# The norm scaling of the scan's head groups, in two halves over items 3 and 4 of the next group

## What is computed

```python
    def finish(yf, yb, xs, z):
        bb, ll = xs.shape[:2]
        y = (yf + flip(yb)).astype(xs.dtype) + xs * d_skip[:, None]
        y = y.reshape(bb, ll, SSD_D_INNER) * jax.nn.silu(z)
        y = rms_norm(y.reshape(bb, ll, SSD_N_GROUPS, SSD_D_INNER // SSD_N_GROUPS),
                     norm_g.reshape(SSD_N_GROUPS, SSD_D_INNER // SSD_N_GROUPS))
        return y.reshape(bb, ll, SSD_D_INNER) @ w_out
```

## Time and profile before

| | us |
|---|---|
| median of 3 runs | 1709.88 |
| the runs | 1709.17 to 1709.90 |
| the profiled execution | 1711.01 |
| its span | 1709.2 |
| TensorE busy | 1544.9 (90%) |
| VectorE busy | 621.9 (36%) |
| ScalarE busy | 373.4 (22%) |
| GpSimd busy | 213.0 (12%) |

### The profile page before, as it was taken

One profiled execution on the slowest core, in us unless ns is written; L12 is line 12 of the kernel. 1 busy time (PEld: TensorE's weight loads), 2 busy tenths in 40 slices (PEclk: granted clock), 3 DMA queues, 4 the chain that ended last, 5 costly groups with the idle time before them and its releaser, 6 DMA issues.

```text
span 1709.2 us, 21638 instructions
## 1 busy us (share of the span) xinstructions
PE 1544.9 (90%) x8512; PEld 788.5 (46%) x8512; DVE 621.9 (36%) x1314; ACT 373.4 (22%) x766; POOL 213.0 (12%) x232
## 2 busy tenths in 40 slices
PE   5999999999999899999888787899999998888886
PEld 2444444555444455545444353445565554444343
DVE  2533447888733414312111111748423211111112
ACT  2311148888610100000000000228210000000000
POOL 2000002222210011010101012111001010101001
PEclk9999999999999999999999999999999999999999
DMA  9687658933489799999999999942599999999997
GB/s 372 253 319 292 256 216 222 321 123 135 145 272 290 251 377 426 425 423 426 425 428 425 428 426 421 355 173 74 218 351 427 423 427 425 425 427 426 426 427 303
DMA packets 145618, 572.71 MB, mean 335 GB/s; under 512 B 23775, under 2 KB 80623, under 8 KB 114688
## 3 DMA queue, kind: packets, MB, share of 16 engines
q1 hardware_dynamic: 124928, 525.25, 77.1%
q0 software_dynamic: 14560, 25.76, 4.2%
q10 hardware_dynamic: 6048, 20.58, 3.5%
HBM read 543.02 MB, written 49.25 MB: 347 GB/s over the span
## 4 chain that ended last, share of the span: by engine, by line
PE 58%; DMA 32%; DVE 6%; issue 2%; ACT 1%; POOL 0%; SPq 0%; ACTq 0%; DVEq 0%; POOLq 0%
DMA mem<-in_moe_w_down_dram 19%; PE bank L2077 13%; DMA mem<-in_moe_w_gate_dram 12%; PE bank L648 9%; PE bank L2092 8%; PE bank L1017 6%; PE bank L962 4%; PE bank L2545 3%; PE bank L386 2%; PE bank L2655 2%; PE bank L984 1%; PE bank L995 1%; DVE mem L1193 1%; PE bank L2063 1%; PE bank L2592 1%
## 5 line engine op out<-in xcount | busy, mean ns | idle before, releaser
L2077 PE MATMUL bank<-mem 128*64 128x256 f32 x4096 | 495.5, 393 | 62.7 <-DMA mem<-in_moe_w_gate_dram 37.5
L2077 PEld LDWEIGHTS bank<-mem 128*64 128x64 f32 x4096 | 284.2, 135 | 271.3 <-DMA mem<-in_moe_w_gate_dram 59.8
L2092 PE MATMUL bank<-mem 128*64 128x512 f32 x1040 | 244.5, 613 | 41.3 <-DMA mem<-in_moe_w_down_dram 37.9
L648 PE MATMUL bank<-mem 128*128 128x512 f32 x384 | 171.2, 598 | 0.2 <-DMA mem<-in_ssd_w_in_dram 0.2
L2278 ACT ACTIVATE mem<-bank 128x256 f32<-128x256 f32 x65 | 24.9, 383 | 662.9 <-PE bank L2077 634.1
L2014 POOL DMA_INDIRECT ys_dram<-mem x61 | 61.2, 1003 | 736.7 <-DVE mem L2360 715.9
L2092 PEld LDWEIGHTS bank<-mem 128*64 128x64 f32 x1040 | 72.5, 140 | 173.7 <-issue 123.4
L2360 DVE TENSOR_TENSOR mem<-bank,mem 128x512 f32<-128x512 f32 x65 | 45.0, 692 | 226.0 <-PE bank L2092 176.0
L2339 DVE TENSOR_TENSOR mem<-mem,bank 128x256 f32<-128x256 f32 x65 | 27.4, 421 | 259.9 <-PE bank L2077 150.4
L648 PEld LDWEIGHTS bank<-mem 128*128 128x128 f32 x384 | 70.8, 190 | 96.9 <-issue 94.9
L962 PE MATMUL bank<-mem 128*128 128x512 f32 x256 | 115.4, 593 | 0.0
(11 more groups left out here) (356 smaller groups left out, 1511.1 us busy)
## 6 DMA issues: line engine op xcount, KB each, us to landing
mem<-in_moe_w_up_dram SPq DMA_DIRECT2D x61, 2048.0 KB, 21.5
mem<-in_moe_w_gate_dram SPq DMA_DIRECT2D x61, 2048.0 KB, 25.8
mem<-in_moe_w_down_dram SPq DMA_DIRECT2D x60, 2048.0 KB, 14.7
mem<-in_mod_w_dram SPq DMA_DIRECT2D x24, 2048.0 KB, 14.7
ys_dram<-consts SPq DMA_DIRECT2D x55, 512.0 KB, 7.5
mem<-in_ssd_w_in_dram SPq DMA_DIRECT2D x10, 2048.0 KB
mem<-ac_dram ACTq DMA_DIRECT2D x32, 512.0 KB, 4.1
mem<-in_ssd_w_out_dram SPq DMA_DIRECT2D x4, 2048.0 KB
```

The lines of the kernel that those rows point to most:

```text
L648: mm = nc.tensor.matmul(psum[c % 2][:, :], lhsT=w[:, k, (c % 4) * P:(c % 4 + 1) * P], rhs=aT[0][:, k, :], start=(k == 0), stop=(k == KD - 1))
L2077: mm = nc.tensor.matmul(bank[half * BR:(half + 1) * BR, 0:HF], lhsT=x[:, k], rhs=w[k][:, half::2], start=(k == 0), stop=(k == KD - 1), ski ...
L2092: mm = nc.tensor.matmul(bank[half * BR:(half + 1) * BR, :], lhsT=ht[:, k // 2, k % 2 * BR:(k % 2 + 1) * BR], rhs=w[:, k, half * COLS:(half ...
```

## The change

`norm` takes the tiles it scales, and is called twice: for tiles 0 and 1 at the end of item 2, for tiles 2 and 3 at the end of item 3. `mean` stays where it was, and the last group's norm too.

```diff
-            def norm(g):
+            def norm(g, tiles=range(NT)):
                 dve.wait_ge(gn_rs, g + 1)
-                for t in range(NT):
+                for t in tiles:
                     y_g = y[:, g % 2, t, :]
                     nc.vector.tensor_scalar(y_g, y_g, grs[:, g, t:t + 1], None, ALU.mult).then_inc(gn_y, 1)
 
...
                 tail(i)
                 if g and k == 1:
                     mean(g - 1)
-                    norm(g - 1)
+                if g and k in (2, 3):
+                    norm(g - 1, range(2 * (k - 2), 2 * (k - 1)))
             mean(GROUPS - 1)
             norm(GROUPS - 1)
```

## The result

The changed kernel takes 1712.34 us against 1709.88 before (medians of 20 runs each). The ratio of the two, taken over all these runs, is 1.0017, with a 95% interval of 1.0009 to 1.0024: 2.9 us slower, between 1.5 and 4.1 us (the medians alone lie 2.5 us apart). The forecast was 1711.5 us, within 0.2% of before, in a range of 1706.5 to 1716.5. The profiled execution's span is 1712.4 us.

A forecast was written before the change was run, and what follows sets the result against it. TensorE bounds the scan, so only its waits for VectorE matter. Groups 2 and 3 add +2.8 us, group 1 gives -1.15: +1.65 us, so 1711.5 us from 1709.88, range 1706.5 to 1716.5.

The forecast's parts named there:

- The trade of waits: Groups 2 and 3: TensorE waits 1.2 us before L979, some 2 before L995, 0.4 before L1008; chance 0.50.
- Ready to turn: TensorE ready for L979 of item 3 to first L1008: 11.39 us in group 2, forecast +1.4 in groups 2 and 3.
- The exponential: ScalarE's L1078 of item 3 ends at 376.61, so L1138 starts about 376.7; 0.9 of almost 6 us left.
- The two stops of item 3: GpSimd's L918 and L925 delay VectorE's L1138 by about 0.4 us and L1141 by 0.8 us.
- The lost collision of item 4: VectorE's L1138 of item 4 comes 0.11 us behind GpSimd's L918 of item 5 and is held up: +0.8 us.
- Group 1: Its clock fall after the 1.87 us wait taken as gone: 13.95 to 12.8 us, so -1.15 us.
- The clock: Scan: group 1's fall to 1.2 GHz, 2.56 us, taken as gone, with no new fall in the main forecast.
- rival C: Longer wait at item 4 lowers the clock over eight L962: +3.4 us per fall, 1714.9 us with one; chance 0.30.
- The signs of being wrong: Wrong if L1138 of item 4 takes 1.23 us, the wait before L979 is gone, or the clock falls elsewhere in scan.

The follow-up runs named there:

- tiny norm: Kernel before with the norms of groups 0 to 2 cut to one column of 512 each; ratio 0.9971 against the kernel before.
- the kernel with L918 held back: Kernel before, GpSimd's power issued after item 3's work, L925 of item 4 right after it, L918 of item 4 held until L1141 of item 3; ratio 0.9952.
- One norm and three: Changed kernel, but one norm after L1183 of item 2 and three after L1183 of item 3; ratio 0.9995 against the kernel before.
- L925 first: Changed kernel with GpSimd's two operations of item 5 in the other order, L925 then L918; ratio 0.9986 against the kernel before.
- one line on GpSimd: Kernel before with GpSimd's power (L936) issued after its work for item 3, not item 1; norms at their old place; ratio 0.9973.
- four after item 2: Changed kernel, but all four norms after L1183 of item 2; ratio 1.0018 against the kernel before.

## Why the prediction was right, and where it was not

**The trade of waits** was right in each step in groups 2 and 3. Predicted in group 2: 1.2 us before L979, some 2 us before L995, 0.4 us before a turn that had never waited. Measured: 1.19, 1.86 and 0.21. Ready to turn grew by 1.32 us in group 2 and 1.35 in group 3, and I had said 1.4.

**The exponential** as what is late next was right: L1138 waited 4.88 us for it, and the tiny norm shows the same 1.19 us before L979. That is why moving the norm away from there gives 0.6 us and not 6. The exponential sets when L1138 starts; nearly all of the 1.19 us that TensorE still waits are the two stops behind it, as the kernel with L918 held back shows (0.1 us).

**The two stops of item 3** were right in sum. L1138 lost 0.44 us and L1141 0.72, where I had 0.4 and 0.8.

**The lost collision of item 4** was right, by 0.09 us for the 0.11 that I had worked out, and worth 0.8 us on VectorE. "One norm and three" and "L925 first" both show it. The Trainium skill (SBUF — State Buffer, "Who interferes with whom") has it that issue order decides and that the loser blocks for the whole instruction. The order agrees. The price does not quite: L918 ran on for 0.95 us after L1138 was issued, and L1138 loses 0.80, as the rows had it.

**Group 1** was the first mis-sized term. I gave it -1.15 us: +1.4 by the waits, as in group 2, and -2.56 for its fall of the clock. It gave -2.3 us (13.95 to 11.65), and -2.56 (to 11.39) in the second profile. The fall behind L979 went as forecast, and the waits cost nothing there. VectorE and TensorE in group 1 of the changed kernel show why:

```profile
323.61 1.35 DVE L1138 TENSOR_TENSOR mem<-mem 128x1024 f32<-128x1024 f32 x1 [3.87 <-ACT mem L1078]
...
327.60 1.12 PE L979 MATMUL bank<-mem 128*128 128x512 f32 x2
337.82 1.78 PE L995 MATMUL bank<-mem 128*128 128x512 f32 x2 [1.86 <-DVE mem L1179]
...
339.00:340.00 1.00, 1.00 (x4) 0.79 (x4) 1.00 (x2) 0.98 (x2) 0.26 (x1) 0.50 0.99 356
```

ScalarE is 1 us earlier against TensorE in group 1: L1138 waits 3.87 us there and 4.88 in group 2, and so L979 waits for nothing. I had taken group 2's exponential for all groups and not read the one of group 1.

**The clock** was the second, and it goes the other way. I let the fall of group 1 vanish without another in its place, and put new falls behind the wait at item 4 into rival C, at 3.4 us each. They came (the row of 339 to 340 us above), and at half that price. In group 2 the time from turn to the next group's ready is 1.74 us longer than in the kernel before. The granted clock of the changed kernel is 0.50 for about 3.4 us each time, where in group 1 of the kernel before it was 6.8 us; I had counted all eight L962 at half clock, and only half of them were (5.29 us for 3.60).

In both profiles of the changed kernel the scan adds up. Ready to turn gives -2.30 + 1.32 + 1.35 = +0.4 us in the first and -2.56 + 1.33 + 1.33 = +0.1 us in the second; behind the turns, where the new falls are, +2.8 and +1.8 us are added. (Group 1's 11.65 us hold 0.26 us of its new fall, which begins while L995 runs.) In all that is +3.2 and +1.9 us, and the measured +2.9 us (1.5 to 4.1) lies there. In the second pair of profiles 1.1 us more came from outside the scan. So the total was near my +1.65 by luck: two errors, of 1.4 us in the waits of group 1 and of 1.8 to 3.1 us in the clock, had different signs.

Sorted by cause, it reads differently. The -2.56 of group 1 is the old fall, not a wait. If 11.39 us is what group 1 of the kernel before takes without its fall, as group 2 does, the waits alone cost 0 + 1.33 + 1.33 = +2.7 us, where I had 1.4 three times. The clock gave 2.56 back and took 1.8 to 3.1, which is between -0.8 and +0.5 us. So the waits are enough for a slower kernel, and the changed kernel need not have had a lower clock than the one before. The mean granted clock of whole executions speaks for this too: it is 0.986 over the 20 runs of the changed kernel and 0.984 over the 73 runs of the kernel before that were taken beside the experiments. How much of the +2.9 us over the 20 runs is the clock's stays open, as only two executions of each kernel were profiled.

**The signs of being wrong.** Of the three signs that I named, one did not come: L1138 of item 4 was stopped, in 2.03 us. Two did: the wait before L979 is gone, in group 1, and the granted clock falls elsewhere in the scan. They mark the two mis-sized terms.

## To carry to other kernels

Before an operation is moved off a path, read what is late next; here an exponential that VectorE had to wait 5 us for left 0.6 us of a gain of 6. Where VectorE and GpSimd both work on memory, the order in which two operations are issued is part of the cost: write both engines' starts as offsets from a common event, and see whose sign the move changes. An operation that looks three times too long may need its rival moved rather than itself; one line on GpSimd gave 4.6 us, and the move of the norm lost 2.9.

## What the runs showed of the hardware

A GpSimd operation of 1.04 us, issued 0.1 to 0.6 us ahead of a VectorE operation on two inputs in memory or of a norm, made that one 0.3 to 0.8 us longer, most where it was only 0.1 us ahead; issued 0.3 us behind it, it was itself 0.8 us longer (1.83 us). Two norms of 0.48 us were stretched to 2.45 us between two GpSimd operations. Operations with one input in a bank (L1160 and L1169) took 0.67 to 0.69 us in all 14 profiles, beside GpSimd or not.

Waits of 1.8 to 1.9 us were followed by 1.2 GHz in one place of the kernel before, the same in both profiles, in two places and then in one other of the changed kernel, and in none of the one profile of "four after item 2". Falls of the granted clock in the scan cost 0 to 3 us in these profiles, and whether one comes can't be read from the waits.
